# Block products with seven multiplications in the down products of two MLPs

## The chip, the cores and the metric

The kernel runs on one core of a Trainium2 chip. The metric is the device time of one execution in microseconds. It is one launch that computes two whole layers; nothing is computed on the host but the order of the weights in memory.

## The reference, cut to what matters

Two layers in float32 over 256 tokens with a model width of 2048. Each has an MLP with a hidden width of 8192 at its end. Only the MLPs are touched:

```python
h = rms_norm(x, norm_mlp_g[l])
x = x + jnp.square(jax.nn.relu(h @ w_mlp_up[l])) @ w_mlp_down[l]      # first layer
...
u = rmsnorm(x, g_mlp) @ w_up
x = x + jnp.square(jax.nn.relu(u)) @ w_down                           # second layer
```

Call the hidden activations A (256 x 8192) and the down weights B (8192 x 2048). A down product is A @ B.

## The kernel before

**Chunks.** All weights lie in one stream of 938 chunks, each 128 partitions x 1024 float32 words (512 KB), in the order in which TensorE uses them. Every product is made in float32 precision from two rounded parts of each operand: with w = whi + wlo and a = hi + lo, three matmuls give hi·whi + hi·wlo + lo·whi. So each chunk goes through four stages. SyncE loads it into one of four slots of `raw` (L462, after `lo_done` says that the slot's last chunk has been split). ScalarE rounds it into `whi` (L553, `prep`; it waits for `mm_done` of the chunk that used the slot of `whi` before, four chunks back). VectorE subtracts, `wlo = raw - whi` (L1023, `prep`). TensorE multiplies after `lo_done`. `prep(c)` prepares chunk c + 4 (`LEAD`), so both engines write the split of a chunk into their instruction order four chunks ahead of its use.

**An MLP** has 4 groups (`FF_GROUPS`). A group makes 16 tiles of 128 hidden units (the function `up`, two chunks each, L1731 and L1732), evacuates each through ScalarE (L758, L762) and VectorE (L1340, L1344, L1347) to a rounded part and a rest in `b_w`, and then adds its part of the down product. That is 32 chunks: for each of four panels of 512 output columns (n = 0 to 3) eight chunks (j = 0 to 7), each with 256 rows of B. A chunk of the down product (`chunk_tok`, L1763 to L1765) is 2 halves of the tokens (h) x 2 row tiles (k) x 3 matmuls, 12 matmuls of 128x512 with 12 weight loads. Panel n accumulates in two banks of PSUM, (pO, pG) for even n and (pS, pT) for odd n, for h = 0 and 1. At the end of a panel VectorE scales and adds both banks to `X` (L1356). The banks acc0, acc1, pV and pN lie idle in the down product; `up` uses acc0 and acc1.

**Order.** There is no planner. Each engine runs its own list of instructions in order, as written in its block, and semaphores tie the lists together. The `up` tiles 2 to 15 run in a loop on each engine; the down product is written out straight.

**Tables.** GpSimd loads `final_g` (fgB), the masks and two cleared tiles into the memory of `branches` once the mixing stage has ended (L518 to L522).

Of the kernel before, what the change touches and what calls it, by code (L numbers as in the profile page):

```python
# [24 lines left out]
F32 = mybir.dt.float32  # L25
# [7 lines left out]
P = 128  # L33
# [66 lines left out]
WI_COL = 64  # L100

# [47 lines left out]
class Semaphores:  # L149


    def __init__(self, make):
# [102 lines left out]
        self.out_landed = make("out_landed")  # L255

# [10 lines left out]
def program(nc, x, x_rows, stream, gates, gateb, finalb, params, consts, onehot, table, bias_scratch, out):  # L267
    with ExitStack() as ctx:
# [149 lines left out]

        acc = [psum("acc0"), psum("acc1")]
# [15 lines left out]
        def pcol(name, k=0):  # L435

            o = PARAMS[name]
            return par[:, ds(k.value(o), 1)] if isinstance(k, At) else par[:, o + k:o + k + 1]

# [45 lines left out]
        def _(pool):  # L485
# [32 lines left out]
            pool.wait_ge(s.t_evac, 2 * G_OUT1)  # L518
# [22 lines left out]
        def _(act):  # L541
            A = nc.scalar.activation

            def prep(c):

                c = c.plus(LEAD)
                if c.least() >= CHUNKS:
                    return
                slot = c.mod(NSLOT)
                act.wait_ge(landed[slot], c.div(NSLOT).times(16).value(16))  # L550
                if c.least() >= NSLOT:
                    act.wait_ge(s.mm_done, c.value(1 - NSLOT))
                A(whi[:, slot, :], raw[:, slot, :], ACT.Copy).then_inc(s.hi_done, 1)  # L553

# [189 lines left out]
            def mlp(b, a, i0, layer, stage, gain, before):  # L744
                for g in range(FF_GROUPS):
                    def up(m):
                        n = m.plus(64 * layer + 16 * g)
                        c, e = m.times(2).plus(b + 64 * g), m.plus(a + 16 * g)
                        first = g == 0 and m.base == 0 and not m.terms
                        if first:  # L750
                            square_x(before, NG - 1, 8 + 24 * layer)
                            norm_hi(stage, NG - 1, gain)
                        prep(c)
                        act.wait_ge(s.mm_done, c.value(2))
                        if n.least() > 0:
                            act.wait_ge(s.up_dve, n.times(2).value())
                        apart(act)
                        A(t1, acc[e.mod(2)][:, T:2 * T], ACT.Copy).then_inc(s.up_copied, 1)  # L758
                        prep(c.plus(1))
                        act.wait_ge(s.up_dve, n.times(2).value(2))  # L760
                        apart(act)
                        A(tile(b_hi, m), t2, ACT.Copy).then_inc(s.hid_hi, 1)  # L762

                    def down(n, last):
                        c, i = At(b + 64 * g + 32 + 8 * n), i0 + 4 * g + n
                        for j in range(8):
                            if last and layer == 0 and n and j in (0, 1):
# [4 lines left out]
                        if last and layer == 1:  # L772
                            for h in range(2):
                                act.wait_ge(s.t_evac, 2 * i + h + 1)
                                act.dma_start(out[:, h, COLS * n:COLS * n + COLS], X[:, h, COLS * n:COLS * n + COLS])\
                                    .then_inc(s.out_landed, 16)

                    up(At(0))
                    up(At(1))
                    with act.Fori(1, 8) as j:  # L780
# [230 lines left out]
        def _(dve):  # L1011
# [4 lines left out]
            def prep(c):  # L1016
# [308 lines left out]

            def mlp(b, a, i0, layer, stage, gain):
                for g in range(FF_GROUPS):
                    def up(m):
# [15 lines left out]
                        STT(t2, t1, 0.0, t1, MAX, MUL).then_inc(s.up_dve, 2)  # L1344
                        prep(c.plus(1))
                        dve.wait_ge(s.hid_hi, n.value(1))
                        TT(tile(b_lo, m), t2, tile(b_hi, m).bitcast(F32), SUB).then_inc(s.hid_ready, 1)  # L1347
# [15 lines left out]
                    up(At(0))  # L1363
                    up(At(1))
                    with dve.Fori(1, 8) as j:
                        up(At(0, (j, 2)))
                        up(At(1, (j, 2)))
                    if layer == 0 and g == FF_GROUPS - 1:
                        dve.wait_ge(s.fg_landed, 16)
                    for n in range(NG):  # L1370
# [347 lines left out]
        def _(pe):  # L1718
# [31 lines left out]
            def chunk_tok(c, i, banks, src, k0, first, last, units=None):  # L1750
# [3 lines left out]
                for h in range(2):  # L1754
# [5 lines left out]
                    for k in range(2):  # L1760
# [4 lines left out]
                        end = MM(ps, lo, wh, start=False, stop=last and k == 1)  # L1765
# [156 lines left out]
            def mlp(b, a, i0, layer, stage, before):  # L1922

                pe.wait_ge(s.t_evac, 2 * before)
                for g in range(FF_GROUPS):
# [8 lines left out]

                    up(At(0))
# [4 lines left out]
                    for n in range(NG):  # L1940
# [321 lines left out]
```

## Time and profile before

| what | value |
| --- | --- |
| time, median of 3 runs | 2694.85 us (2694.68 to 2695.68) |
| time of the profiled execution | 2694.8 us |
| its span, from the first to the last instruction | 2692.9 us |
| TensorE matmul / weight load busy | 100% / 84% |
| VectorE / ScalarE busy | 63% / 48% |
| granted clock of TensorE | 1.00 |
| HBM over the span | 189 GB/s |

The time is that of the execution as the device reports it, 1.9 us more than the span of its trace. Busy shares are averages over the span. The matmuls are pipelined, so a matmul's duration is longer than the distance to the next one; what a matmul costs is read from the distance of two starts. For VectorE and ScalarE, too, the start of the next instruction can lie a little before the modelled end of the one before.

### The profile page before, as it was taken

What the parts mean: (1) busy time and instruction counts of PE and PEld (TensorE: products, weight loads), DVE (VectorE), ACT (ScalarE), POOL (GpSimd) and SP (SyncE); (2) the same over time, 40 slices, a digit from 0 to 9 for tenths busy, and PEclk for the clock granted to TensorE, in tenths of its full rate; (3) what the DMA queues carried; (4) which work ended last, traced back from release to release, by engine and by line L of the source; (5) the groups of instructions that cost most, each with busy time, mean ns of one, the idle gap of its engine ahead of it and who ended that gap; (6) DMA issues with size and microseconds to landing.
All of it is one profiled execution on the core that took longest, in us unless ns stands there. A gap on an engine that the chain in (4) does not pass through costs nothing.

```text
span 2692.9 us, 39858 instructions
## 1 busy us (share of the span) xinstructions
PE 2683.9 (100%) x13616; PEld 2267.7 (84%) x13616; DVE 1705.9 (63%) x2422; ACT 1296.7 (48%) x1791; POOL 30.4 (1%) x64
## 2 busy tenths in 40 slices
PE   9999999999999999999999999999999999999999
PEld 7888888888888888888888888888888888888887
DVE  6687876555555655655656567878776565565564
ACT  6455555444445544534434554556554344453443
POOL 0100000000000000000000000000000000000000
PEclk9999999999999999999999999999999999999999
DMA  8655656665665555555555555545555655555555
GB/s 278 228 180 177 192 170 194 203 200 197 200 210 186 186 187 190 186 194 188 188 194 187 187 182 163 179 150 188 170 181 187 195 188 187 190 185 195 188 187 171
DMA packets 141710, 510.98 MB, mean 190 GB/s; under 512 B 16134, under 2 KB 16439, under 8 KB 141464
## 3 DMA queue, kind: packets, MB, share of 16 engines
q1 hardware_dynamic: 136312, 493.86, 55.9%
q0 software_dynamic: 3840, 12.86, 1.5%
q10 hardware_dynamic: 1440, 2.62, 0.3%
q8 instruction: 81, 1.33, 0.2%
q14 instruction: 37, 0.30, 0.0%
HBM read 505.08 MB, written 4.21 MB: 189 GB/s over the span
## 4 chain that ended last, share of the span: by engine, by line
PE 98%; DVE 1%; ACT 0%; issue 0%; DMA 0%; SPq 0%; DVEq 0%; ACTq 0%
PE acc L1731 26%; PE acc L1732 13%; PE acc L1746 5%; PE pS L1763 4%; PE pS L1765 4%; PE pT L1763 4%; PE pS L1764 4%; PE pT L1765 4%; PE pT L1764 4%; PE acc L1763 4%; PE acc L1765 4%; PE acc L1764 4%; PE pO L1763 2%; PE pO L1765 2%; PE pO L1764 2%; PE pG L1765 2%
## 5 line engine op out<-in xcount | busy, mean ns | idle before, releaser
L1023 DVE TENSOR_TENSOR wlo<-raw,whi 128x1024 fp32r<-128x1024 f32 x938 | 1146.6, 1224 | 751.0 <-ACT whi L553 747.7
L553 ACT ACTIVATE whi<-raw 128x1024 fp32r<-128x1024 f32 x938 | 991.7, 1058 | 922.2 <-PE pT L1765 335.9
L1731 PE MATMUL acc<-a_w,whi 128*128 128x512 f32 x2944 | 1046.2, 400 | 0.1
L1732 PE MATMUL acc<-a_w,wlo 128*128 128x256 f32 x2944 | 826.7, 281 | 0.0
L1731 PEld LDWEIGHTS acc<-a_w,whi 128*128 128x128 f32 x2944 | 553.3, 188 | 138.2 <-issue 0.8
L1732 PEld LDWEIGHTS acc<-a_w,wlo 128*128 128x128 f32 x2944 | 556.2, 189 | 0.7
L1746 PE MATMUL acc<-a_w,whi 128*128 128x512 f32 x592 | 214.7, 404 | 0.0
L1747 PE MATMUL acc<-a_w,wlo 128*128 128x256 f32 x592 | 165.8, 280 | 0.0
L758 ACT ACTIVATE t<-acc 128x256 f32<-128x256 f32 x128 | 49.1, 384 | 235.0 <-PE acc L1732 235.0
L1340 DVE TENSOR_TENSOR t<-acc,t 128x256 f32<-128x256 f32 x128 | 54.4, 425 | 125.5 <-ACT t L758 125.4
L1746 PEld LDWEIGHTS acc<-a_w,whi 128*128 128x128 f32 x592 | 111.2, 188 | 26.9 <-issue 2.0
L1763 PE MATMUL pS<-whi,b_w 128*128 128x512 f32 x320 | 125.7, 393 | 0.0
L1764 PE MATMUL pS<-wlo,b_w 128*128 128x512 f32 x320 | 124.6, 389 | 0.0
L1765 PE MATMUL pS<-whi,b_w 128*128 128x512 f32 x320 | 124.6, 389 | 0.0
L1763 PE MATMUL pT<-whi,b_w 128*128 128x512 f32 x320 | 124.5, 389 | 0.0
L1765 PE MATMUL pT<-whi,b_w 128*128 128x512 f32 x320 | 124.5, 389 | 0.0
L1764 PE MATMUL pT<-wlo,b_w 128*128 128x512 f32 x320 | 124.5, 389 | 0.0
L1747 PEld LDWEIGHTS acc<-a_w,wlo 128*128 128x128 f32 x592 | 111.9, 189 | 0.3
L1763 PE MATMUL acc<-whi,a_w 128*128 128x512 f32 x256 | 100.0, 391 | 2.2 <-DVE wlo L1023 2.2
L1763 PE MATMUL pO<-whi,b_w 128*128 128x512 f32 x256 | 99.8, 390 | 0.0
L1764 PE MATMUL pO<-wlo,b_w 128*128 128x512 f32 x256 | 99.7, 389 | 0.0
L1765 PE MATMUL acc<-whi,a_w 128*128 128x512 f32 x256 | 99.6, 389 | 0.0
(420 smaller groups left out, 3402.1 us busy)
## 6 DMA issues: line engine op xcount, KB each, us to landing
raw<-stream SPq DMA_DIRECT2D x938, 512.0 KB, 3.3
gbias<-gateb POOLq DMA_DIRECT2D x12, 256.0 KB, 3.7
X<-x_rows POOLq DMA_DIRECT2D x4, 512.0 KB, 6.3
bias_scratch<-brow POOLq DMA_DIRECT2D x8, 256.0 KB, 5.6
q<-bias_scratch POOLq DMA_DIRECT2D x8, 256.0 KB, 4.2
out<-X ACTq DMA_DIRECT2D x8, 256.0 KB, 4.7
xF<-x SPq DMA_DIRECT2D x6, 256.0 KB, 6.5
bias<-bias_scratch POOLq DMA_DIRECT2D x8, 128.0 KB, 3.9
```

Source lines behind the costliest of these rows:

```text
L553: A(whi[:, slot, :], raw[:, slot, :], ACT.Copy).then_inc(s.hi_done, 1)
L758: A(t1, acc[e.mod(2)][:, T:2 * T], ACT.Copy).then_inc(s.up_copied, 1)
L1023: TT(wlo[:, slot, :], raw[:, slot, :], whi[:, slot, :].bitcast(F32), SUB).then_inc(s.lo_done, 1)
L1340: TT(t1, acc[e.mod(2)][:, 0:T], t1, ADD).then_inc(s.evacuated, 1)
L1731: MM(ps, wh, wide[:, k0 + k, :], start=start and k == 0, stop=False, skip_group_check=True)
L1732: last = MM(ps[:, 0:T], wl, wide[:, k0 + k, 0:T], start=False, stop=not start and k == KC - 1, skip_group_check=True)
L1746: MM(ps, wh, a_w[:, m, :], start=half == 0 and k == 0, stop=False, skip_group_check=True)
L1747: last = MM(ps[:, 0:T], wl, a_w[:, m, 0:T], start=False, stop=half == 1 and k == KC - 1, skip_group_check=True)
L1763: MM(ps, hi, wh, start=first and k == 0, stop=False)
L1764: MM(ps, hi, wl, start=False, stop=False)
L1765: end = MM(ps, lo, wh, start=False, stop=last and k == 1)
```

## The change

In seven of the eight groups (all but the last of the first MLP), the panels 0 and 1 are computed together, in eight steps of two chunks (one for each panel, the same 256 rows of B). Steps 4, 5, 6 and 7 are as before. Steps 0, 1, 2 and 3 are seen as 2 x 2 blocks: A has the blocks a(h, r) of 128 tokens x 128 hidden units, B has the blocks b(r, e) of 128 x 512. Eight block products are replaced by seven, on sums of blocks (Winograd's form of Strassen's scheme). The order of the steps is 4, 0, 5, 1, 6, 2, 7, 3.

VectorE makes the four sums of each pair of chunks (`weight_sums`; three go to `sums`, one takes the place of b(0, 1) in `raw`), and from the hidden tiles 0 to 7 the four sums of each pair of tiles (`mixed_tiles`). ScalarE and VectorE split them into rounded part and rest, as everything else. Three of the seven products (and the ordinary steps) accumulate in pO, pS, pG, and four (M1, and the ones that several output blocks share) in acc0, pN, acc1 and pV. In the middle of panel 2, ScalarE copies acc0 and VectorE combines the four banks (`block_parts`) and adds the four results to `X` (`block_add`). The final evacuation of panels 0 and 1 is in `corner`. Panels 2 and 3 are as before. The `up` tiles 0 to 7, 14 and 15 of such a group are written out on ScalarE and VectorE, in place of the loop; on TensorE the loop stays. TensorE waits in a block step for each chunk, for the mixed tiles and for the sums separately. The tables of GpSimd are loaded after the third block group has been added. The output of panels 0 and 1 is written with that of panel 2. In the stream, chunks of the two panels alternate.

The diff, cut to its core and, where it lies deep, with eight columns of indentation less:

```diff
--- before.py
+++ after.py
@@ -98,6 +98,17 @@
 N_PARAMS = _at
 DT_ROW = 96
 WI_COL = 64
+BLOCK_GROUPS = [(0, 0), (0, 1), (0, 2), (1, 0), (1, 1), (1, 2), (1, 3)]
+N_BLOCK = 4
+LATE_OUT = 2 if (1, 3) in BLOCK_GROUPS else 0
+BLOCK_ORDER = (4, 0, 5, 1, 6, 2, 7, 3)
+BLOCK_CHUNKS = {}
+for _p, (_l, _g) in enumerate(BLOCK_GROUPS):
+    for _j in range(N_BLOCK):
+        for _e in range(2):
+            BLOCK_CHUNKS[(B_MLP2 if _l else B_MLP1) + 64 * _g + 32 + 2 * BLOCK_ORDER.index(_j) + _e] = (N_BLOCK * _p + _j, _e)
...
 rg = take("rg", 8)[:, 0:4].rearrange("p (g h) -> p g h", h=2)
+sums = sb("sums", 3 * COLS, F32, at=at_br)[0]
+sums_hi = sb("sums_hi", 6 * COLS, F32R, at=at_br + 12 * COLS)[0].rearrange("p (k c) -> p k c", k=2)
+sums_lo = sb("sums_lo", 6 * COLS, F32R, at=at_br + 36 * COLS)[0].rearrange("p (k c) -> p k c", k=2)
+mixed_hi = sb("mixed_hi", N_BLOCK * COLS, F32R, at=at_br + 60 * COLS)[0].rearrange("p (k c) -> p k c", c=COLS)
+mixed_lo = sb("mixed_lo", 4 * COLS, F32R, at=at_br + (60 + 4 * N_BLOCK) * COLS)[0].rearrange("p (k c) -> p k c", c=COLS)
+mixed_lo = [mixed_lo[:, k, :] for k in range(4)]
...
-    pool.wait_ge(s.t_evac, 2 * G_OUT1)
+    pool.wait_ge(s.m_added, 4 * 3)
...
+        k, second = (None, 0) if c.terms else BLOCK_CHUNKS.get(c.base, (None, 0))
+        if second:
+            act.wait_ge(s.sums_made, k + 1)
         A(whi[:, slot, :], raw[:, slot, :], ACT.Copy).then_inc(s.hi_done, 1)
+        if second:
+            if k >= 2:
+                act.wait_ge(s.block_done, k - 1)
+            A(sums_hi[:, k % 2, :], sums, ACT.Copy).then_inc(s.sums_hi, 1)
...
-                A(tile(b_hi, m), t2, ACT.Copy).then_inc(s.hid_hi, 1)
+                part = block_tile(p, m)
+                A(tile(b_hi, m), even if part == 0 else t2, ACT.Copy).then_inc(s.hid_hi, 1)
+                if part == 1:
+                    act.wait_ge(s.mixed_made, N_BLOCK * p + m.base // 2 + 1)
+                    A(mixed_hi[:, m.base // 2, :], mixed, ACT.Copy).then_inc(s.mixed_hi, 1)
...
+                    if p is not None and n == 2 and j == 1:
+                        act.wait_ge(s.block_done, N_BLOCK * p + N_BLOCK)
+                        if p:
+                            act.wait_ge(s.m_added, 4 * p)
+                        apart(act)
+                        A(m1, acc[0], ACT.Copy).then_inc(s.m1_copied, 1)
...
+                if last and layer == 1 and n >= LATE_OUT:
+                    if n == LATE_OUT and p is not None:
+                        act.wait_ge(s.m_added, 4 * p + 4)
+                    for r in range(n if n > LATE_OUT else 0, n + 1):
+                        for h in range(2):
+                            act.wait_ge(s.t_evac, 2 * (i - n + r) + h + 1)
+                            act.dma_start(out[:, h, COLS * r:COLS * r + COLS], X[:, h, COLS * r:COLS * r + COLS])\
+                                .then_inc(s.out_landed, 16)
...
+            fixed = 2 if p is None else 2 * N_BLOCK
+            for m in range(fixed):
+                up(At(m))
+            with act.Fori(fixed // 2, 8 if p is None else 7) as j:
                 up(At(0, (j, 2)))
                 up(At(1, (j, 2)))
+            if p is not None:
+                up(At(14))
+                up(At(15))
...
         slot = c.mod(NSLOT)
+        k, second = (None, 0) if c.terms else BLOCK_CHUNKS.get(c.base, (None, 0))
+        if k is not None and not second:
+            weight_sums(c.base, slot, k)
         dve.wait_ge(s.hi_done, c.value(1))
         TT(wlo[:, slot, :], raw[:, slot, :], whi[:, slot, :].bitcast(F32), SUB).then_inc(s.lo_done, 1)
+        if second:
+            if k >= 2:
+                dve.wait_ge(s.block_done, k - 1)
+            dve.wait_ge(s.sums_hi, k + 1)
+            TT(sums_lo[:, k % 2, :], sums, sums_hi[:, k % 2, :].bitcast(F32), SUB).then_inc(s.sums_lo, 1)
+    def weight_sums(c, slot, k):
+        for e in range(2):
+            dve.wait_ge(landed[slot + e], 16 * ((c + e) // NSLOT + 1))
+        if k:
+            dve.wait_ge(s.sums_hi, k)
+            dve.wait_ge(s.sums_lo, k)
+        b11, b21 = raw[:, slot, 0:COLS], raw[:, slot, COLS:]
+        b12, b22 = raw[:, slot + 1, 0:COLS], raw[:, slot + 1, COLS:]
+        d1, d2, d4 = (sums[:, COLS * e:COLS * e + COLS] for e in range(3))
+        TT(d1, b12, b11, SUB).then_inc(s.sums_step, 1)
+        dve.wait_ge(s.sums_step, 3 * k + 1)
+        TT(d2, b22, d1, SUB).then_inc(s.sums_step, 1)
+        TT(b12, b22, b12, SUB).then_inc(s.sums_step, 1)
+        dve.wait_ge(s.sums_step, 3 * k + 3)
+        TT(d4, b21, d2, SUB).then_inc(s.sums_made, 1)
     def evac(a, dst):
...
             xg = X[:, h, COLS * n:COLS * n + COLS]
             TT(xg, xg, fgB[:, COLS * n:COLS * n + COLS], MUL).then_inc(s.x2_done, 1)
+    def mixed_tiles(j, k, tiles):
+        a11, a21, a12, a22 = even[:, 0:P], even[:, P:T], t2[:, 0:P], t2[:, P:T]
+        s1, s2, s3, s4 = (mixed[:, P * e:P * e + P] for e in range(4))
+        dve.wait_ge(s.up_dve, 2 * tiles)
+        if k:
+            dve.wait_ge(s.mixed_ready, k)
+        TT(s1, a21, a22, ADD).then_inc(s.mixed_step, 1)
+        TT(s3, a11, a21, SUB).then_inc(s.mixed_step, 1)
+        dve.wait_ge(s.mixed_step, 3 * k + 2)
+        TT(s2, s1, a11, SUB).then_inc(s.mixed_step, 1)
+        dve.wait_ge(s.mixed_step, 3 * k + 3)
+        TT(s4, a12, s2, SUB).then_inc(s.mixed_made, 1)
+        dve.wait_ge(s.mixed_hi, k + 1)
+        TT(mixed_lo[j], mixed, mixed_hi[:, j, :].bitcast(F32), SUB).then_inc(s.mixed_ready, 1)
+    def block_parts(p):
+        dve.wait_ge(s.m1_copied, p + 1)
+        dve.wait_ge(s.block_done, N_BLOCK * p + N_BLOCK)
+        if p:
+            dve.wait_ge(s.m_added, 4 * p)
+        TT(u2, pV, m1, ADD).then_inc(s.m_step, 1)
+        dve.wait_ge(s.m_step, 3 * p + 1)
+        TT(u3, pN, u2, ADD).then_inc(s.m_step, 1)
+        dve.wait_ge(s.m_step, 3 * p + 2)
+        TT(u2, acc[1], u2, ADD).then_inc(s.m_step, 1)
+        TT(u4, acc[1], u3, ADD).then_inc(s.m_free, 1)
+    def block_add(p, e, i):
+        dve.wait_ge(s.t_evac, 2 * i + 4)
+        dve.wait_ge(s.m_step, 3 * p + 3)
+        dve.wait_ge(s.m_free, p + 1)
+        for h, part in ((0, u2 if e else m1), (1, u4 if e else u3)):
+            xg = X[:, h, COLS * e:COLS * e + COLS]
+            STT(xg, part, rsq[:, h:h + 1], xg, MUL, ADD).then_inc(s.m_added, 1)
     def mlp(b, a, i0, layer, stage, gain):
         for g in range(FF_GROUPS):
+            p = block_group(layer, g)
             def up(m):
                 n = m.plus(64 * layer + 16 * g)
...
+                if part == 1:
+                    mixed_tiles(m.base // 2, N_BLOCK * p + m.base // 2, n.value(1))
...
+                def corner(e, h):
+                    xg = X[:, h, COLS * e:COLS * e + COLS]
+                    STT(xg, tbanks(At(i + e), True)[h], rsq[:, h:h + 1], xg, MUL, ADD).then_inc(s.t_evac, 1)
+                for t in range(16):
+                    if t == 14:
+                        dve.wait_ge(s.t_half, i + 1)
+                        corner(0, 0)
+                    if t == 15:
+                        dve.wait_ge(s.block_corner, p + 1)
+                        corner(0, 1)
+                        dve.wait_ge(s.t_half, i + 2)
+                        corner(1, 0)
+                        corner(1, 1)
+                    prep(At(c + t))
...
+                    if p is not None and n == 2 and j == 2:
+                        block_parts(p)
+                    if p is not None and n == 2 and j in (4, 5):
+                        block_add(p, j - 4, i0 + 4 * g)
...
         end.then_inc(s.mm_done, 1)
+    def block_step(c, k, i, g, layer):
+        slot, j, p = c % NSLOT, k % N_BLOCK, k // N_BLOCK
+        first, last = j == 0, j == N_BLOCK - 1
+        d1, d2, d4 = ([w[:, k % 2, COLS * e:COLS * e + COLS] for w in (sums_hi, sums_lo)] for e in range(3))
+        s1, s2, s3, s4 = ([w[:, P * e:P * e + P] for w in (mixed_hi[:, j, :], mixed_lo[j])] for e in range(4))
+        a = lambda r, h: [b_w[:, 2 * j + r, T * w + P * h:T * w + P * h + P] for w in range(2)]
+        w = lambda e, r: [x[:, slot + e, COLS * r:COLS * r + COLS] for x in (whi, wlo)]
+        c11, c21 = tbanks(At(i), True)
+        c12 = tbanks(At(i + 1), True)[0]
+        def product(ps, left, right, fresh=False):
+            MM(ps, left[0], right[0], start=fresh, stop=False)
+            MM(ps, left[0], right[1], start=False, stop=False)
+            return MM(ps, left[1], right[0], start=False, stop=last)
+        pe.wait_ge(s.mixed_ready, k + 1)
+        pe.wait_ge(s.lo_done, c + 1)
+        end = product(c11, a(1, 0), w(0, 1))
+        if last:
+            end.then_inc(s.t_half, 1)
+        if first:
+            pe.wait_ge(s.evacuated, (A_MLP2 if layer else A_MLP1) + 16 * g + 16)
+            if p:
+                pe.wait_ge(s.m_free, p)
+        product(acc[0], a(0, 0), w(0, 0), first).then_inc(s.mm_done, 1)
+        pe.wait_ge(s.lo_done, c + 2)
+        end = product(c12, s4, w(1, 1))
+        if last:
+            end.then_inc(s.t_half, 1)
+        product(pN, s3, w(1, 0), first).then_inc(s.mm_done, 1)
+        pe.wait_ge(s.sums_lo, k + 1)
+        end = product(c21, a(1, 1), d4)
+        if last:
+            end.then_inc(s.block_corner, 1)
+        product(acc[1], s1, d1, first)
+        product(pV, s2, d2, first).then_inc(s.block_done, 1)
...
+            p = block_group(layer, g)
+            before_p = block_group(layer, g - 1)
+            if before_p is not None:
+                pe.wait_ge(s.m_free, before_p + 1)
...
-            for n in range(NG):
+            for t in range(0 if p is None else 8):
+                c, k, i = b + 64 * g + 32 + 2 * t, BLOCK_ORDER[t], i0 + 4 * g
+                if k < N_BLOCK:
+                    block_step(c, N_BLOCK * p + k, i, g, layer)
+                    continue
+                pe.wait_ge(s.hid_ready, 64 * layer + 16 * g + 2 * k + 2)
+                for e in range(2):
+                    chunk_tok(At(c + e), At(i + e), tbanks(At(i + e), True), b_w, 2 * k, t == 0, False,
+                              corner=t == 6 and e == 1)
+            for n in range(0 if p is None else 2, NG):
...
+    if (layer, g) in BLOCK_GROUPS:
+        for k in BLOCK_ORDER:
+            yield d[0:2, 8 * g + k]
+        yield d[2:4, 8 * g:8 * g + 8]
+    else:
+        yield d[:, 8 * g:8 * g + 8]
```

Not shown: the names of the new semaphores, `even` as the place of the even hidden tiles 0 to 7 before they are rounded, the same unrolling on VectorE as on ScalarE (with `down_pair()` at its end), and the flag `corner` of `chunk_tok`, which only marks the end of an accumulation.

## Rows read from the trace of the kernel before

**Rows 1.** Page, part 1: busy time, share of the span, instructions of each engine

```profile
PE 2683.9 (100%) x13616; PEld 2267.7 (84%) x13616; DVE 1705.9 (63%) x2422; ACT 1296.7 (48%) x1791; POOL 30.4 (1%) x64
```

**Rows 2.** Page, part 4: the chain that ended last, by engine

```profile
PE 98%; DVE 1%; ACT 0%; issue 0%; DMA 0%; SPq 0%; DVEq 0%; ACTq 0%
```

**Rows 3.** Waits: engine, line, waited for: us in total, times, longest

```profile
DVE wlo L1023 <- ACT whi L553: 747.7, 633, 2.7
...
ACT whi L553 <- PE pT L1765: 335.9, 215, 2.8
...
PE acc L1763 <- DVE wlo L1023: 2.2, 1, 2.2
```

**Rows 4.** Timeline of matmuls, first down group: start us, us, what

```profile
973.55 0.39 PE L1765 MATMUL pG<-whi,b_w 128*128 128x512 f32 x1
973.78 0.39 PE L1763 MATMUL pO<-whi,b_w 128*128 128x512 f32 x1
...
979.22 0.39 PE L1763 MATMUL pO<-whi,b_w 128*128 128x512 f32 x1
...
981.94 0.39 PE L1763 MATMUL pO<-whi,b_w 128*128 128x512 f32 x1
```

**Rows 5.** Windows: panels 1 to 3; PE, PEld, DVE, ACT, POOL, PEclk, DMA share, GB/s

```profile
990.10:1055.38 65.28, 65.28 (x290) 54.05 (x289) 33.37 (x31) 25.45 (x24) 0.00 (x0) 1.00 0.60 194
```

**Rows 6.** Groups by line: busy us, mean ns | idle before, releaser

```profile
L1023 DVE TENSOR_TENSOR wlo<-raw,whi 128x1024 fp32r<-128x1024 f32 x938 | 1146.6, 1224 | 751.0 <-ACT whi L553 747.7 <-DVE tsm L1524 0.3 <-DVE tsm L1072 0.2
...
L553 ACT ACTIVATE whi<-raw 128x1024 fp32r<-128x1024 f32 x938 | 991.7, 1058 | 922.2 <-PE pT L1765 335.9 <-PE pG L1765 222.8 <-PE acc L1732 163.2
...
L762 ACT ACTIVATE b_w<-t 128x256 f32 (+1 forms) x128 | 53.6, 419 | 33.4 <-DVE t L1344 31.8
...
L567 ACT ACTIVATE sq<-X 128x512 f32<-128x512 f32 x40 | 25.0, 625 | 5.4 <-DVE X L1682 4.7
...
L1492 DVE TENSOR_TENSOR gth<-gth,cbt 128x768 f32<-128x768 f32 x8 | 7.6, 955 | 2.3 <-ACT gth L856 2.3
...
L1324 DVE TENSOR_TENSOR X<-X,xs 128x512 f32<-128x512 f32 x8 | 5.2, 686 | 0.0
...
L1129 DVE TENSOR_SCALAR L<-L,small 128x128 f32<-128x128 f32 x16 | 4.6, 287 | 0.6
```

**Rows 7.** Timeline of VectorE, from the last `up` tiles to panel 1

```profile
963.30 0.42 DVE L1340 TENSOR_TENSOR t<-acc,t 128x256 f32<-128x256 f32 x1 [0.99 <-ACT t L758]
963.83 0.42 DVE L1344 SCALAR_TENSOR_TENSOR t<-t 128x256 f32<-128x256 f32 x1
964.25 1.23 DVE L1023 TENSOR_TENSOR wlo<-raw,whi 128x1024 fp32r<-128x1024 f32 x1
965.39 0.42 DVE L1347 TENSOR_TENSOR b_w<-t,b_w 128x256 f32 x1
...
968.97 0.42 DVE L1340 TENSOR_TENSOR t<-acc,t 128x256 f32<-128x256 f32 x1 [1.00 <-ACT t L758]
...
989.87 0.75 DVE L1356 SCALAR_TENSOR_TENSOR X<-pO,tsm,X 128x512 f32<-128x512 f32 x1
990.53 0.74 DVE L1356 SCALAR_TENSOR_TENSOR X<-pG,tsm,X 128x512 f32<-128x512 f32 x1
```

**Rows 8.** Timeline of ScalarE in panel 0

```profile
974.03 1.06 ACT L553 ACTIVATE whi<-raw 128x1024 fp32r<-128x1024 f32 x1 [1.66 <-PE pG L1765]
```

**Rows 9.** SyncE's loads (L462) from 968 to 1060 us, 34 of them

```profile
DMA to landing us min/median/max: 3.2/3.3/4.0
```

**Rows 10.** Timeline of VectorE, third tile of the first MLP

```profile
894.00 1.23 DVE L1023 TENSOR_TENSOR wlo<-raw,whi 128x1024 fp32r<-128x1024 f32 x1
895.46 0.42 DVE L1340 TENSOR_TENSOR t<-acc,t 128x256 f32<-128x256 f32 x1 [0.24 <-ACT t L758]
```

**Rows 11.** Timeline, the last instructions of the kernel

```profile
2688.32 0.75 DVE L1356 SCALAR_TENSOR_TENSOR X<-pS,tsm,X 128x512 f32<-128x512 f32 x1 [7.14 <-PE pS L1765]
...
2689.68 0.75 DVE L1356 SCALAR_TENSOR_TENSOR X<-pT,tsm,X 128x512 f32<-128x512 f32 x1 [0.61 <-PE pT L1765]
```

More of the change, by code:

```diff
@@ L417, in program @@
         rg = take("rg", 8)[:, 0:4].rearrange("p (g h) -> p g h", h=2)
+        sums = sb("sums", 3 * COLS, F32, at=at_br)[0]
[4 more added lines that the diff above has]
+        mixed_lo = [mixed_lo[:, k, :] for k in range(4)]
+        take = under(at_gth, 6 * T)
+        even, mixed = take("even", T), take("mixed", COLS)
+        take = under(at_wk, 9 * T)
+        m1, u2, u3, u4 = (take(n, COLS) for n in ("m1", "u2", "u3", "u4"))
         acc = [psum("acc0"), psum("acc1")]
@@ L438, in pcol, with block_group, block_tile @@
             return par[:, ds(k.value(o), 1)] if isinstance(k, At) else par[:, o + k:o + k + 1]
+        def block_group(layer, g):
+            return BLOCK_GROUPS.index((layer, g)) if (layer, g) in BLOCK_GROUPS else None
+        def block_tile(p, m):
+            return m.base % 2 if p is not None and not m.terms and m.base < 2 * N_BLOCK else None
         def apart(eng):
@@ L771, in down @@
                                 norm_hi(2, n - 1, "g_mix2")
[L772 to L780, printed above, removed]
+                        if last and layer == 1 and n >= LATE_OUT:
[10 more added lines that the diff above has]
+                    with act.Fori(fixed // 2, 8 if p is None else 7) as j:
                         up(At(0, (j, 2)))
                         up(At(1, (j, 2)))
+                    if p is not None:
+                        up(At(14))
+                        up(At(15))
                     for n in range(NG):
@@ L1361, in down @@
                                 turned_lo(2, n - 1, "g_mix2")
-                    up(At(0))
-                    up(At(1))
-                    with dve.Fori(1, 8) as j:
+                    fixed = 2 if p is None else 2 * N_BLOCK
+                    for m in range(fixed):
+                        up(At(m))
+                    with dve.Fori(fixed // 2, 8 if p is None else 7) as j:
                         up(At(0, (j, 2)))
                         up(At(1, (j, 2)))
+                    if p is not None:
+                        up(At(14))
+                        up(At(15))
+                        down_pair()
                     if layer == 0 and g == FF_GROUPS - 1:
                         dve.wait_ge(s.fg_landed, 16)
-                    for n in range(NG):
+                    for n in range(0 if p is None else 2, NG):
                         down(n, g == FF_GROUPS - 1)
@@ L1748, in half_unit, with chunk_tok @@
                 last.then_inc(s.mm_done, 1)
-            def chunk_tok(c, i, banks, src, k0, first, last, units=None):
+            def chunk_tok(c, i, banks, src, k0, first, last, units=None, corner=False):
                 slot = c.mod(NSLOT)
@@ L1764, in chunk_tok @@
                         MM(ps, hi, wl, start=False, stop=False)
-                        end = MM(ps, lo, wh, start=False, stop=last and k == 1)
+                        end = MM(ps, lo, wh, start=False, stop=(last or (corner and h == 1)) and k == 1)
                     if last and h == 0:
@@ L1939, in mlp @@
                         up(At(1, (j, 2)))
-                    for n in range(NG):
+                    for t in range(0 if p is None else 8):
[7 more added lines that the diff above has]
+                                      corner=t == 6 and e == 1)
+                    for n in range(0 if p is None else 2, NG):
                         i = At(i0 + 4 * g + n)
@@ L2193, with mlp @@
     parts += [panels(a["w_out"][0])]
-    def mlp(up, down):
+    def mlp(layer, up, down):
         u, d = blocks(up), panels(down)
```

28 lines of the change are left out of this document (23 added, 5 removed).

## The prediction

> **What bounds the kernel now.** I read the page first. TensorE is busy for the whole span, at the full granted clock, and no other engine is above 63% [rows 1, 5]. The chain of waits says the same: 98% of the time to the last instruction is TensorE's own work [rows 2]. Then the waits: VectorE waits for ScalarE, and ScalarE for TensorE to be done with a slot; in the other direction one wait of 2.2 us, once in the kernel, is the largest on a chunk [rows 3]. So preparing weights is a race that TensorE never loses, and time can only be won by giving TensorE fewer matmuls. The third view is the timeline: what a matmul really takes. Its "0.39 us" overlaps with the next. Two starts twelve matmuls apart are 981.94 - 979.22 = 2.72 us, 226.7 ns each [rows 4]. Panels 1 to 3, 288 matmuls, take 65.28 us, again 226.7 ns [rows 5].
>
> **What the change removes.** A block step has 7 products x 3 = 21 matmuls of 128x512 where 2 chunks had 24. There are 7 groups x 4 = 28 such steps, so 84 matmuls go: 84 x 0.2267 = 19.0 us, if TensorE stays fed. The seven products have the old shape, with a full 128x128 weight load each, and change bank every 3 matmuls instead of every 6. A change of bank, and of chunk, costs nothing in the rows: 973.55 to 973.78 is a normal step, with a wait for the chunk and one for hidden tiles on the matmul [rows 4]. I give the block matmuls 226.7 ns; the ends are 215 and 240 ns (5% for banks or waits, 588 matmuls, +7.8 us at worst), and I take the row that is the same instruction.
>
> The Trainium skill gives a shorter distance for N = 512 at the full clock ("TensorE: Matmul & The Clock Gate", Back-to-back issue gap: N / 2.4 + 2.5 ns, 215.8 ns). By it the 84 matmuls would be worth 18.1 us as an estimate, and the time 2676.7. The trace disagrees by 11 ns in every such pair of starts, so the row decides.
>
> **What it adds, and what lies over it.** All of it is on VectorE and ScalarE; the question is whether they still arrive in time. First durations. VectorE's float32 operations lie on a line: 287, 686, 955, 1224 ns for 128, 512, 768, 1024 words [rows 6], 1.04 ns a word and 154 ns. The split of the three sums (1536 words) isn't in the trace: the line gives 1.75 us, the bounds are 1.22 (as for 1024) and 2.45 (twice 1024). ScalarE: 419 ns for 256 words and 1058 for 1024 [rows 6] give 1.48 us for 1536. Starts of independent instructions lie 0.09 us closer than their duration (989.87 to 990.53 for 0.75; 964.25 to 965.39 for 1.23), of dependent ones 0.11 us further (963.30 to 963.83 for 0.42) [rows 7].
>
> Now one pair, from the first sum. The sums start at 0, 0.79, 1.39, 2.18 and are made at 2.87. `wlo` of the first chunk runs to 4.0. ScalarE, which has waited for the sums, rounds the second chunk from 2.97 to 4.03 and the sums to 5.42; VectorE splits the second chunk to 5.36 and the sums from 5.52 to 7.28. The two ordinary chunks behind them take 1.14 each, so the list is through at 9.5 us. TensorE's time for these four chunks is now 5.44 + 4.76 = 10.20 us (12 x 2 and 21 matmuls), before 10.88. VectorE goes to 93% here, and is not the bound.
>
> The lead is the other half. ScalarE starts on a chunk 0.25 us after TensorE left its slot (974.03 against 973.78) [rows 4, 8]. Call S the start of a block step. The ordinary chunk ahead of the next pair's sums is released at S, rounded at S + 1.31, split at S + 2.58; so the sums start at S + 2.5, the first chunk is split at S + 6.5, the second at 7.9, the sums at 9.8. TensorE wants them in the next step at S + 10.2, 11.56 (after 6 matmuls) and 12.92 (after 12). The least margin is 3.1 us. This is where the split waits count: with one wait at the head of the step the margin would be 0.4.
> - Loads: the slot of a pair's second chunk is free once the pair before has been split (5.36 after its first sum), and 3.3 us later, 4.0 at most, the load has landed [rows 9]; that is 8.7 to 9.4, of 10.2 that are there.
> - First pair of a group: its sums lie ahead of the evacuation of tile 15, 2.8 us later than before. TensorE needs acc1 and acc0 only after two ordinary chunks, 5.4 us on. Covered.
> - Corners: the four evacuations move to the end of the pair stretch. VectorE does `corner(0, 0)` to S + 3.2 and `corner(0, 1)` to S + 5.0 in the last step; panel 2 needs pG at S + 4.76 + 1.36 = 6.12. Margin 1.1 us, the smallest of all.
> - Middle of panel 2: four operations on PSUM and four additions to X, some 6 us of VectorE in three chunks, where it is idle half of the time (33.4 of 65.3 us busy [rows 5]); behind them wait only splits with four chunks of lead. The banks are free 35 us before `up` wants them.
> - Mixed tiles, 4 per group: four operations of 287 ns, one of ScalarE (0.63) and one of 686 ns, with handovers some 2.7 us per two tiles. A tile takes 5.67 us (L1340 at 963.30 and 968.97) and keeps VectorE busy for 3 x 0.42 + 2 x 1.23 = 3.7 [rows 7], so two tiles leave 3.9 idle. ScalarE's next rounding comes 2.3 us late, against a lead of three chunks. The tightest is tile 1 of each MLP, behind the norm's small steps: the split at 894.00 moves some 3 us, to end at 898.2. TensorE wants that chunk when tile 3 is done, a tile's 5.7 us after tile 2, whose evacuation begins at 895.46 [rows 10]: about 900.4. Covered, by 2 us.
> - Tables: 1.25 MB now load near 1390 us instead of at 788, wanted at 1525. Some loads beside them may land late, in a stretch of ordinary chunks. Nothing.
> - The unrolled tiles add instructions to lists that wait anyway; TensorE's list gets shorter. The last panel and its evacuation [rows 11] stay; the outputs of panels 0 and 1 go out some 20 us ahead of the end.
>
> **Sum.** Profiled execution 2694.8 (span 2692.9, 1.9 outside it, unchanged): -19.0 gives 2675.8. The median of the runs is 0.05 higher, so it is the same forecast: 2675.8 us, -0.71%.
>
> **Rivals.**
> - *The sums come late in part* (about 10%). VectorE's pair takes more than 10.2 us: handovers between three engines that I put at 0.1 us, or loads that land in pairs. From 1.1 us of delay on, the bank pG is late for panel 2, or the sums for the step. One to three us in each of 7 groups: 2683 to 2690 less the margin, I take 2684. Against it: each step has 0.7 us of spare time to catch up.
> - *Waits cost TensorE time* (5%). A block step has two to four waits more than two chunks had. If each of some 3 x 28 = 84 held the array for as long as a dependent start does on VectorE (0.11 us [rows 7]), 9 us of the gain would go at most; half of that gives 2680. For it the Trainium skill: an instruction that waits for several engines can have a separate semaphore instruction put in front of it ("Perfetto Trace Analysis", Identifying Dependency Chains). By that rule the list grows here; the trace shows no mark of such an instruction in the first chunk of the down product, where both kinds of wait stand.
> - *Slower: VectorE becomes the bound* (5%). One mechanism: float32 operations on three streams, or of 1536 words, cost twice their line beside the matmul's reads. The pair's own 4.5 us (four sums and their split) become 9, the list 14.1 us per 10.2. Three periods and the margin: 3 x 3.9 - 3.1 = 8.6 us lost per group, against 2.7 won: 7 x 5.9 = +41 us, 2736. It beats the gain from a list of about 12.1 us on, 1.6 times the rows' price. Against it, four sizes lie on one line while TensorE runs at full pace.
> - *The block matmuls aren't shorter in sum* (2%): a bank change every 3 matmuls costs what the 84 give, 19 / 588 = 32 ns each. 2695. The rows show nothing of the kind.
>
> **How the numbers follow.** The main case has 0.78 and its own range is 2674.8 to 2677. Partly late sums 0.10, waits 0.05, slower 0.05, no change 0.02. The range 2674.4 to 2682 takes in the main case and the lower part of the two small losses and leaves out some 0.15. A measurement of this kernel can tell 0.2% (5.4 us) from no change: faster is the main case, the waits and nearly all of the late sums, 0.92; same 0.03 and slower 0.05.
>
> **What would show it.** Right: TensorE has 84 instructions less (13532) and stays at 100%; no wait of TensorE in the down products; starts in a block step 226.7 ns apart; each of the seven groups 2.72 us shorter and all other stages the same. VectorE some 220 us busier (per group 4 x 4.5 for the pairs, 7.3 mixed, 5.7 combining), ScalarE some 60. The distance from the last split of sums to the matmul that uses it about 3 us. Wrong: gaps before the product on d4 (the sums late), before the first pG matmul of panel 2 (the corners late), or at the head of each block step (loads or waits). If VectorE shows no idle time through the pair stretch and the stretch is longer than 43.5 us less 2.7, the slow rival holds.

## The result and the profile after

The changed kernel takes 2676.34 us, median of 4 runs (2676.01 to 2677.86), beside 2694.95 us of the kernel before on the same chip (2694.68 to 2695.68): ratio 0.9931, 95% interval 0.9919 to 0.9943. The forecast was 2675.8. The profiled execution has a span of 2674.7 us, 18.2 less than before.

Parts 1 and 4 of its page (for [rows 1, 2]):

```profile
PE 2665.4 (100%) x13532; PEld 2252.3 (84%) x13532; DVE 1899.7 (71%) x2758; ACT 1349.8 (50%) x1854; POOL 30.3 (1%) x64
...
PE 98%; DVE 1%; ACT 0%; DMA 0%; issue 0%; SPq 0%; DVEq 0%; ACTq 0%
```

TensorE has exactly the 84 matmuls fewer and is as full as before. All waits of TensorE that the view of waits lists for the whole span, with engine, line, what for, us in total, times, longest (for the last line of [rows 3]):

```profile
PE acc L1930 <- DVE wlo L1096: 2.5, 1, 2.5
PE pV L2048 <- POOL L L533: 1.5, 1, 1.5
PE pT L1996 <- DVE L L1225: 1.4, 2, 0.8
PE pN L2205 <- ACT irelu L882: 0.5, 1, 0.5
```

None of them lies in an MLP; each stood in the trace before, in the same place, the first with 2.2 us. So where did the 18.2 us come from? ScalarE's copy `t <- acc` marks every `up` tile. From tile 15 of one group to tile 0 of the next it was 92.71 to 92.74 us in all six pairs of groups before, and is 89.99 to 90.02 now: 2.72 us less, which is 12 matmuls x 0.2267 = 2.72. The way through a group's 16 tiles is 84.80 to 84.82 in both. Seven groups give 19.0. Of the 0.8 that is missing in the span, 0.54 arose ahead of the first MLP (first copy at 884.27 against 883.73) and 0.25 between the two MLPs, where the code is the same.

The prices that [rows 6] didn't have, from the groups by line:

```profile
L1101 DVE TENSOR_TENSOR sums_lo<-sums,sums_hi 128x1536 fp32r<-128x1536 f32 x28 | 49.2, 1756 | 4.5 <-ACT sums_hi L604 4.5
L604 ACT ACTIVATE sums_hi<-sums 128x1536 fp32r<-128x1536 f32 x28 | 41.2, 1473 | 0.0
L1435 DVE TENSOR_TENSOR mixed_lo<-mixed,mixed_hi 128x512 fp32r<-128x512 f32 x28 | 19.4, 693 | 19.5 <-ACT mixed_hi L819 19.5
L1115 DVE TENSOR_TENSOR sums<-raw,sums 128x512 f32<-128x512 f32 x28 | 19.4, 692 | 1.0
L1433 DVE TENSOR_TENSOR mixed<-t,mixed 128x128 f32<-128x128 f32 x28 | 8.2, 292 | 1.0
```

1756 and 1473 ns were put at 1.75 and 1.48 us. Now the race itself: VectorE's list over one period of the pair stretch (the eight steps of panels 0 and 1) of the first group, and the start of the pG product that needs the sums (timelines, start us, us, what):

```profile
987.00 0.68 DVE L1113 TENSOR_TENSOR sums<-raw 128x512 f32<-128x512 f32 x1
987.72 0.69 DVE L1115 TENSOR_TENSOR sums<-raw,sums 128x512 f32<-128x512 f32 x1
988.33 0.69 DVE L1116 TENSOR_TENSOR raw<-raw 128x512 f32<-128x512 f32 x1
989.05 0.69 DVE L1118 TENSOR_TENSOR sums<-raw,sums 128x512 f32<-128x512 f32 x1
989.66 2.52 DVE L1096 TENSOR_TENSOR wlo<-raw,whi 128x1024 fp32r<-128x1024 f32 x2
992.40 1.76 DVE L1101 TENSOR_TENSOR sums_lo<-sums,sums_hi 128x1536 fp32r<-128x1536 f32 x1 [0.22 <-ACT sums_hi L604]
994.08 1.22 DVE L1096 TENSOR_TENSOR wlo<-raw,whi 128x1024 fp32r<-128x1024 f32 x1
996.06 1.23 DVE L1096 TENSOR_TENSOR wlo<-raw,whi 128x1024 fp32r<-128x1024 f32 x1 [0.77 <-ACT whi L600]
997.20 0.69 DVE L1113 TENSOR_TENSOR sums<-raw 128x512 f32<-128x512 f32 x1
```

```profile
994.71 0.39 PE L1949 MATMUL pO<-whi,b_w 128*128 128x512 f32 x1
...
997.43 0.39 PE L1949 MATMUL pG<-sums_hi,b_w 128*128 128x512 f32 x1
```

From 987.00 to 997.20 the list repeats in 10.20 us, TensorE's period, and is idle for 0.22 + 0.77 of it. The split of the sums is done at 994.16; the step starts at 994.71 and needs it at 997.43. The lead is 3.3 us, of which one wait at the head would have left 0.55. In the down products of the block groups, from the last `up` tile of a group on, no two starts of matmuls lie more than 0.24 us apart.

### The profile page after: what moved, and what is told of

It reads as the page before. It is cut to its first block, busy times and chain, and to the rows that moved or that the text cites. A ratio compares the mean times of both kernels' runs of the same rounds, so it can differ in the third digit from the quotient of the medians.

```text
span 2674.7 us, 39556 instructions
## 1 busy us (share of the span) xinstructions
PE 2665.4 (100%) x13532; PEld 2252.3 (84%) x13532; DVE 1899.7 (71%) x2758; ACT 1349.8 (50%) x1854; POOL 30.3 (1%) x64
## 4 chain that ended last, share of the span: by engine, by line
PE 98%; DVE 1%; ACT 0%; DMA 0%; issue 0%; SPq 0%; DVEq 0%; ACTq 0%
PE acc L1898 26%; PE acc L1899 13%; PE acc L1913 5%; PE acc L1930 4%; PE acc L1932 4%; PE acc L1931 4%; PE pS L1930 3%; PE pS L1932 3%; PE pS L1931 3%; PE pT L1932 3%; PE pT L1930 3%; PE pT L1931 3%; PE acc L1914 2%; PE pO L1930 2%; PE pO L1931 2%; PE pO L1932 2%
## 5 line engine op out<-in xcount | busy, mean ns | idle before, releaser
L600 ACT ACTIVATE whi<-raw 128x1024 fp32r<-128x1024 f32 x938 | 991.2, 1058 | 831.8 <-PE pT L1932 283.3
L1930 PE MATMUL pS<-whi,b_w 128*128 128x512 f32 x264 | 103.9, 394 | 0.0
L1932 PE MATMUL pS<-whi,b_w 128*128 128x512 f32 x264 | 102.8, 389 | 0.0
L1931 PE MATMUL pS<-wlo,b_w 128*128 128x512 f32 x264 | 102.8, 389 | 0.0
L1930 PE MATMUL pT<-whi,b_w 128*128 128x512 f32 x264 | 102.8, 389 | 0.0
L1932 PE MATMUL pT<-whi,b_w 128*128 128x512 f32 x264 | 102.7, 389 | 0.0
L1931 PE MATMUL pT<-wlo,b_w 128*128 128x512 f32 x264 | 102.7, 389 | 0.0
L1931 PE MATMUL acc<-wlo,a_w 128*128 128x512 f32 x256 | 99.6, 389 | 0.0
L1930 PE MATMUL pO<-whi,b_w 128*128 128x512 f32 x200 | 78.0, 390 | 0.0
```

Of the source, the lines that this page charges most:

```text
L1930: MM(ps, hi, wh, start=first and k == 0, stop=False)
L1931: MM(ps, hi, wl, start=False, stop=False)
L1932: end = MM(ps, lo, wh, start=False, stop=(last or (corner and h == 1)) and k == 1)
```

## The experiments

The baselines are 2694.9 to 2695.0 for the kernel before, which was timed again beside the variants, and the 2676.3 of the change from its own series; the change was not timed again with them.

**The eighth product put back.**

```diff
-                product(pV, s2, d2, first).then_inc(s.block_done, 1)
+                product(pV, s2, d2, first, open_=True)
+                product(pV, s2, d2).then_inc(s.block_done, 1)
```

> Every block step gets an eighth block product (the one into pV is made twice, so that bank's share of the result is doubled); all work of VectorE, ScalarE and the DMA queues and all waits of the change stay. Theory (TensorE is the bound, the preparation is wholly hidden, and each of the 84 matmuls is worth its 226.7 ns): 19.0 us come back, 2676.3 + 19.0 = 2695.4, within 0.5 us of the kernel before (2694.95); what is above it is the price of waits, handovers and tables. Rival 'waits cost TensorE time': 2697 to 2704. Rival 'the gain came from another thing than the matmuls' (order of the stream, unrolling, tables): clearly under 2694.

Measured: 2695.03 us (2693.93 to 2696.45, 11 runs), ratio to the kernel before 1.0002 (0.9993 to 1.0011). The way from group to group is 92.69 to 92.74 us again. With all sums, splits, semaphores and moved tables in place, the kernel costs what the kernel before costs: the gain is the matmuls alone, and the waits of TensorE cost nothing that can be measured. This run has TensorE's old period of 10.88 us again, so it doesn't show that the preparation also fits into 10.20; that is shown by the trace of the change.

**One wait at the head of the step.**

```diff
-                pe.wait_ge(s.lo_done, c + 1)
+                pe.wait_ge(s.lo_done, c + 2)
+                pe.wait_ge(s.sums_lo, k + 1)
                 end = product(c11, a(1, 0), w(0, 1))
```

> TensorE waits for both chunks and the sums at the head of each block step instead of in three places. In the trace of the changed kernel the split of the sums of the later pairs ends 0.55 to 0.6 us before the head of its step and the first pair of a group 0.13 us before it. Theory (TensorE doesn't feel waits that are already met): no change, 2676.3, at most 0.1 us for the first step of each group, 2677.0. Rival (the split waits are what makes the step work, as the margins of 3.1 against 0.4 us in the prediction may suggest once loads scatter): some 0.5 us per step, 2680 to 2690. If waits as such cost TensorE time, this kernel is faster than the change.

Measured: 2676.23 us (2674.66 to 2676.33, 5 runs), and its view of waits lists none of TensorE in the MLPs. Once, at the first block step of the first group, two starts lie 0.37 and 0.31 us apart (972.25, 972.62, 972.92) instead of 0.23: 0.2 us, where 0.1 was allowed for. In the later steps the 0.55 us ahead of the head are enough, and the time did not change. The split waits are a reserve, and not what makes the step work.

**Three block steps in a row.**

```diff
-BLOCK_ORDER = (4, 0, 5, 1, 6, 2, 7, 3)
+BLOCK_ORDER = (4, 0, 1, 2, 5, 6, 7, 3)
```

> The same steps in the order 4, 0, 1, 2, 5, 6, 7, 3: three block steps back to back; the work of every engine in sum is the same. VectorE needs 7.1 us per block step (4 sums, 2 splits, split of the sums), TensorE 4.76. Theory (a race of VectorE's list against TensorE with some 3 us of lead): the first and second step fit, the third waits for its first chunk by 1.9 us and for its sums by 0.5: 2.4 us per group, 7 groups: 16.7 us, 2693. The waits show on the first matmul of the third step. Rival (only the average load of VectorE in the stretch counts, 93%): no change, 2676.3.

Measured: 2691.50 us (2691.25 to 2694.53, 11 runs), +15.2. Waits of TensorE in this run's trace:

```profile
PE pO L1949 <- DVE wlo L1096: 10.2, 7, 1.7
...
PE pG L1949 <- DVE sums_lo L1101: 1.3, 7, 0.2
```

Once per group each, on the first product of the third step and on the one that needs the sums, 1.46 and 0.19 us on average where 1.9 and 0.5 were forecast. The view counts such a wait from the modelled end of the matmul before, 0.39 us after its start, though the next one would have started 0.23 after it. Read from the distances of starts, the two places cost 1.7 to 1.9 and 0.45 to 0.47 us, which is near the forecast and gives the 2.2 to 2.5 us by which the way from group to group grew. The work is the same in sum, and four fifths of the gain are gone: the order of the steps carries it.

**More work for VectorE**, 1.14 us per pair of chunks, and twice that:

```diff
+                if second:
+                    TT(spare, raw[:, slot, :], whi[:, slot, :].bitcast(F32), SUB)
                 TT(wlo[:, slot, :], raw[:, slot, :], whi[:, slot, :].bitcast(F32), SUB).then_inc(s.lo_done, 1)
```

> One more VectorE operation of 128x1024 per pair of chunks, into an unused place (1.14 us in the list; the result is as before). VectorE's list per two steps goes from 9.5 us plus 0.2 us of handovers to about 10.5, over TensorE's 10.20. Theory (lead and margins as in the prediction): the delay that gathers over four pairs reaches the last evacuation, bank pG is late for panel 2 by 0.4 us in each group: 2676.3 + 2.7 = 2679.0, and no wait before a block step. Rival 'VectorE is already the bound': 28 x 1.14 = +32 us, 2708. Rival 'there are several us of room': no change.

> Two more VectorE operations of 128x1024 per pair of chunks into unused places (2.28 us in the list; the result is as before). The traces of the change and of the run with one extra operation give VectorE's list as 9.2 us of work per two steps, 1.0 idle, 10.2 TensorE. With two extras the list needs 11.3 to 11.5. Theory (beyond about 1.1 us per pair every further one is paid): the margins are used up after the first pairs, then waits of 0.3 to 0.7 us at the second chunk and the sums of each step and 1.3 us at panel 2, 4.2 to 4.4 us per group: 2676.3 + 30 = 2706, so the kernel before is beaten by 11 us. Rival (VectorE paid in full once it is the bound): 28 x 2.28 = +64, 2740. Rival (room is larger than thought): under 2685.

Measured: one extra 2675.66 us (2675.52 to 2676.18), no change; two extras 2705.88 us (2704.37 to 2705.96), +29.5, 4.2 to 4.6 us from group to group (94.2 to 94.6 against 90.0). In the first the extra took the place of the idle time: the list has no gap, and its period is 10.16 us (first sums at 987.58 and 997.74). The last evacuations of the pair stretch came at

```profile
1007.90 0.74 DVE L1496 SCALAR_TENSOR_TENSOR X<-pO,tsm,X 128x512 f32<-128x512 f32 x1
1008.56 1.21 DVE L1099 TENSOR_TENSOR wlo<-raw,whi 128x1024 fp32r<-128x1024 f32 x1
1009.70 0.74 DVE L1496 SCALAR_TENSOR_TENSOR X<-pG,tsm,X 128x512 f32<-128x512 f32 x1
```

and panel 2's first matmul on pG at 1010.61, 0.17 after the second of them. My forecast of +2.7 counted the handovers of 0.2 us on top of the extra operation, though it covers them. The list is full with one extra, so it has some 1.1 us of room per pair. The second extra, 28 x 1.14 = 32 us, was paid in nearly full. The waits of the run with two are

```profile
PE pS L1953 <- DVE wlo L1100: 7.4, 15, 0.5
PE pO L1934 <- DVE X L1497: 4.8, 7, 0.7
```

and the distances of starts show the rest: in the first group, 1.3 us go at the banks of panel 2, as expected, and 3.1 us at the second chunk (0.7 to 0.8 us each) and the sums (0.3) of the three later block steps.

**The parts that don't touch the matmuls**, in the kernel before: the late tables and the unrolled tiles.

```diff
-            pool.wait_ge(s.t_evac, 2 * G_OUT1)
+            pool.wait_ge(s.t_evac, 2 * (G_MLP1 + 11))
...
-                    up(At(0))
-                    up(At(1))
-                    with dve.Fori(1, 8) as j:
+                    for m in range(8):
+                        up(At(m))
+                    with dve.Fori(4, 7) as j:
```

> The kernel before with only the late tables (GpSimd waits for panel 2 of the third group) and the `up` tiles 0 to 7, 14, 15 written out on ScalarE and VectorE in all eight groups. Theory (both are hidden): 2694.9, within 0.5. Rival (0.5 us of the change's shortfall against the forecast are from these): 2695.4 to 2696.

Measured: 2695.00 us (2693.56 to 2696.85, 10 runs), ratio 1.0001 (0.9991 to 1.0011). Nothing, as forecast.

**Five steps of eight.** `N_BLOCK = 5`, order 5, 0, 6, 1, 2, 7, 3, 4, and a place for the fifth `mixed_lo`.

> Five of eight steps as block steps, order 5, 0, 6, 1, 2, 7, 3, 4: 28 - 7 fewer x 3 = 105 matmuls removed instead of 84, 4.8 us more if TensorE stays fed (2671.5). VectorE gets 4.5 us more in a stretch of 40.1 us in which it had 4 us idle. Theory (VectorE's list is the limit of this scheme in one column half): the delay at the end of the stretch shows as a wait of panel 2 for its evacuated banks, 0.9 us for pO and 0.4 for pG, and some 0.1 before sums: net +0.8 us per group, 2681.6; four of eight is the best number. Rival (enough room): 2671.5 to 2674.

Measured: 2691.02 us (2689.33 to 2691.30, 10 runs). The verdict (four is better) held, the size did not: +2.1 us per group where +0.8 was forecast. Its waits:

```profile
PE pO L1949 <- DVE wlo L1096: 4.8, 7, 1.2
PE pO L1930 <- DVE X L1493: 4.6, 7, 0.7
...
PE pG L1949 <- DVE sums_lo L1101: 1.1, 7, 0.2
```

The last pair's first chunk is late by 0.7 us per group as the view counts it, and by 1.0 in the starts of the first group, which I hadn't forecast. VectorE's list shows a part of the reason:

```profile
990.87 2.35 DVE L1096 TENSOR_TENSOR wlo<-raw,whi 128x1024 fp32r<-128x1024 f32 x2
993.61 0.69 DVE L1113 TENSOR_TENSOR sums<-raw 128x512 f32<-128x512 f32 x1 [0.39 <-issue]
```

The slot of the second chunk came free when a split ended at 988.97, and the sums started 4.64 us later. With pairs side by side, slots come free in bursts, and SyncE's loads took a median of 4.1 us to land (964 to 1016 us) where the change has 3.4 (968 to 1012). The load into that slot was issued at 989.14 and landed at 993.53, 0.08 us before the sums started, so the 0.39 us, which the trace calls "issue", are the wait for it. That the bursts make the loads longer isn't shown: in both stretches a load issued 1.3 us behind another took 4.0 to 4.5 us, but in panels 2 and 3 of the change, where they are 2.7 us apart, the median is 4.3 too (1022 to 1058 us), beside 3.3 in the kernel before [rows 9]. Behind 993.61 the list has no gap over 0.23 us until the late chunk is split, so the 0.39 us reach it in full; the rest of the 1.0 isn't divided up here. The sums, too, came later than I had put them: 0.4 us in the distances of starts, against 0.1.

**The version that the runs point to: the second column half too.** VectorE is at its limit in the pair stretch, and idle for more than a third of the panels 2 and 3 (in the change it is busy for 27.0 us of the 43.0 from 1012.0 on). The new units and their orders:

```diff
-BLOCK_ORDER = (4, 0, 5, 1, 6, 2, 7, 3)
+STEPS = (4, 3)
+BLOCK_ORDER = ((4, 0, 5, 1, 6, 2, 7, 3), (3, 4, 5, 0, 6, 1, 7, 2))
+UNITS = [(l, g, half) for l, g in BLOCK_GROUPS for half in range(2) if half == 0 or (l, g) != (1, 3)]
...
+                    if before_u is not None:
+                        pe.wait_ge(s.m1_copied, before_u + 1)
                     up(At(0))
+                    if before_u is not None:
+                        pe.wait_ge(s.m_free, before_u + 1)
                     up(At(1))
...
+                    if before_u is not None:
+                        block_parts(before_u)
+                    for m in range(16):
+                        if before_u is not None and 8 <= m < 12:
+                            corner(before_u, i0 + 4 * g - 2, (m - 8) // 2, m % 2)
+                        if before_u is not None and m >= 12:
+                            block_add(before_u, (m - 12) // 2, i0 + 4 * g - 2, (m % 2,))
+                        up(At(m))
```

ScalarE copies acc0 right after the second product of the unit's last step, so that `up` can start in it.

> The version that the runs point to. Panels 2 and 3 of six groups (not the last of either MLP) also in block form, with 3 of 8 steps (order 3, 4, 5, 0, 6, 1, 7, 2), which leaves VectorE time for the combining of the first half behind its first chunks; the second half's combining comes at the start of the next `up`, its eight additions to X one by one ahead of the tiles 8 to 15, all 16 tiles written out on VectorE. 18 more block steps: 54 more matmuls fewer, 12.2 us. Theory (VectorE's list stays ahead: about 37 us of 41.5 in the new stretch, some 12 us more in the `up` stretch that has 31 idle): 2676.3 - 12.2 = 2664.1, no new wait of TensorE. Rival (acc0 and acc1 are not free in time for the first two tiles of the next `up`): 0.5 to 2 us in each of six groups, 2667 to 2676. Rival (VectorE late in the second stretch): slower than 2676.

Measured: 2664.28 us (2664.02 to 2665.67, 4 runs), ratio to the kernel before 0.9888 (0.9872 to 0.9905), 12.1 us less than the change has. The way from group to group is 87.95 to 87.98 us. Windows of the pair stretch, the second one and the next `up` (us, busy us and count of PE, PEld, DVE, ACT, POOL, clock, DMA share, GB/s):

```profile
968.00:1009.00 41.00, 41.00 (x183) 33.93 (x182) 37.34 (x40) 23.90 (x23) 0.00 (x0) 1.00 0.62 203
1009.00:1050.00 41.00, 41.00 (x182) 33.97 (x181) 38.53 (x42) 21.68 (x21) 0.00 (x0) 1.00 0.61 200
1050.00:1141.00 91.00, 91.00 (x515) 78.92 (x514) 71.04 (x111) 45.30 (x66) 0.00 (x0) 1.00 0.56 190
```

VectorE is busy for 91% and 94% of the two stretches, and TensorE never waits in an MLP. This kernel and the change were each timed against the kernel before, not against each other.

## Why the prediction was right

- *The bound.* TensorE's own matmuls, at a distance of 226.7 ns. Shown from both sides: 84 fewer give 2.72 us per group, 84 put back take it all away, and 54 fewer again give 2.04 us per group for 9 matmuls (89.99 to 87.95), 227 ns each. By the 215.8 ns of the Trainium skill ("TensorE: Matmul & The Clock Gate", Back-to-back issue gap), which the section calls the gap of an isolated matmul and not that of a stream like this one, the 84 would have given 18.1 us; the groups gave 19.0.
- *The sum.* -19.0 was forecast; it is -19.0 in the groups, -18.2 in the span, -18.6 in the medians. What lies between groups and span is scatter of stages that the change doesn't touch: over the traces in which the clock stayed at 1.00, the first copy lies anywhere from 883.7 to 884.4. The time outside the span, put at 1.9 us and unchanged, was 1.6 in the profiled execution of the change. So the forecast missed by 0.5 us: 0.8 of scatter against it, and 0.2 to 0.3 outside the span in its favour, by chance and not by the sum.
- *The list of 9.5 us per 10.2.* It takes 9.4 us with its wait of 0.22 for ScalarE, and has 9.2 us of work. The four sums took 2.66 us to the first split, 2.78 forecast.
- *The margins.* Sums 3.1 us forecast, 3.3 measured; 0.4 and 0.55 at the head. Bank pG for panel 2: 1.1 forecast; in the trace its evacuation ends at 1009.95 and the matmul starts at 1011.03. The late split behind the norm: forecast end 898.2, trace 898.4, with the stage 0.5 later. None was used up in the trace of the change. The bank's margin was called the smallest of all, but the loads had less: the load of a pair's second chunk, issued at 992.35, took 4.3 us, where at most 4.0 was put, and landed at 996.62, 0.6 us before the sums at 997.20; 0.8 to 1.5 was forecast.
- *The rivals.* "Waits cost TensorE time" falls with the eighth product (2695.03). What the prediction says of the separate semaphore instructions is wrong: the trace of the kernel before holds records of them on TensorE, 51 ns each, which the views leave out, one in that first chunk (at 969.70 us) and the next in the second (at 972.44). They cost nothing: the matmuls on either side of the one at 972.44 start at 972.42 and 972.64. And there are hardly more of them after the change, 352 in the kernel for 346.
- *The slow rival.* "VectorE becomes the bound" is a true mechanism with a wrong price here: its operations cost what the line says, and the edge lies 1.1 us per pair further on. I had put the turn to slower than before at a list of 12.1 us; two extras gave 11.3 (first sums at 989.89 and at 1001.19) and were slower already. By the formula they would have lost 3 x 1.1 - 3.1 = 0.2 us per group, and lost 4.2 to 4.6. It charged the margin only with what a period has over 10.2 us. But a pair's own splits stand behind its extra operations, so the second pair is late by its own 2.28 us and by the 1.3 that the first pair's outran the idle time, 3.6 in all (an estimate from these rows), and the margin was gone by then: TensorE's first wait of the run lies in the second block step.
- *Busy times.* VectorE rose by 194 us, not 220, as an instruction that starts under the end of the one before counts once for the overlap; ScalarE by 53, forecast 60. Added up one by one, VectorE's instructions are 218 us more.

## What to carry to other kernels

When TensorE is full, price a removed matmul by the distance of two starts in that very stage, and then ask only whether the engines that pay for it keep their lead: add up one period of the list of each, and find the smallest time between an item being ready and being wanted. Charge that smallest time with all the extra work that lies ahead of the item, and not only with what the period is too long. Put the costly steps between cheap ones: three of them together cost 15 us here at the same mean load. Before adding more to a list that is 90% full, look for a second stretch where the same engine idles: five steps in one half cost 15 us, three in the other half won 12.

## What was not expected of the hardware

- One `up` stage, with the same instructions, has two paces. In two of the traces above (the eighth product and the one wait), the way from tile 0 to tile 15 of the first group was 83.22 us, in all others 84.82, and TensorE kept its pace for the whole stage. In a window of 20 us (columns as above), in the change:

```profile
900.00:920.00 20.00, 20.00 (x115) 17.32 (x114) 16.39 (x30) 11.47 (x17) 0.00 (x0) 1.00 0.64 206
```

and in the run with one wait:

```profile
900.00:920.00 20.00, 20.00 (x117) 17.66 (x116) 16.87 (x31) 11.40 (x18) 0.00 (x0) 1.00 0.60 202
```

Two matmuls more fit into the same 20 us, and the granted clock is 1.00 in both. What sets the pace stays open. These two executions were the shortest of their kernels, 1.1 and 1.6 us below the median, so the pace may be the lower end of the spread of the kernel before (2693.04 to 2697.32). The upper end is another thing: a stretch of lower clock at the very start. The profiled execution of the kernel with the late tables, 2696.82 us, has (columns as above)

```profile
10.00:15.00 5.00, 5.00 (x17) 4.01 (x16) 3.68 (x6) 3.42 (x7) 0.00 (x0) 0.69 1.05 394
```

where the kernel before has

```profile
10.00:15.00 5.00, 5.00 (x23) 3.99 (x22) 4.03 (x6) 3.45 (x7) 0.00 (x0) 1.00 1.05 393
```

From 10.0 to 13.0 us the clock is 0.50, the lower of its two levels (1.2 GHz of 2.4), and the starts lie 0.43 us apart; just before, TensorE had waited 2.0 us for a split, as it does in the other traces, where the clock stays. That costs 1.6 us. Wherever runs of a kernel have a mean clock of 0.999, they are its longest, 1.4 to 3.0 us above the median.
- A TensorE wait costs 0.24 to 0.28 us more than the view of waits says. Of it, 0.16 is the way of counting (from the modelled end of the matmul before, 0.39 after its start, and not from 0.23). The rest comes behind the wait: the first matmul reads 0.47 or 0.50 us instead of 0.39, and the next starts 0.31 or 0.34 later instead of 0.23 (run of five steps, 1004.94 to 1005.25 and 1008.13 to 1008.47).
